# A list scheduler that weighs the remaining chain, and earlier gates for the first weight slabs

## The reference, cut to what matters

```python
def reference(x, ...):                                   # x: (4, 4096, 1024) float32, one layer
    h = rmsnorm(x, norm_mix_g)
    q, f, i, g, c_gate, b_gate, xb, gate_a, gate_b = jnp.split(h @ w_in, offsets, axis=-1)
    y_a = hgrn2_mixer(q, f, i, g, lb, hg_norm_g) @ w_branch_a    # gated linear recurrence, 4 heads,
                                                                 # state 128 x 128 per head
    y_b = (b_gate * causal_conv3(c_gate * xb)) @ w_branch_b
    x = x + (sigmoid(gate_a) * y_a + sigmoid(gate_b) * y_b) @ w_out
    h2 = rmsnorm(x, norm_ffn_g)
    x = x + (silu(h2 @ w_ffn_gate) * (h2 @ w_ffn_up)) @ w_ffn_down       # hidden width 2816
    return rmsnorm(x, norm_final_g)
```

## Time and profile before

| | |
|---|---|
| time, median of 3 runs (lowest to highest) | 1033.21 us (1032.44 to 1033.33) |
| the profiled execution's own time | 1035.37 us |
| its span, slowest core (core 3) | 1033.8 us |
| spans of the eight cores | 1024.6 to 1033.8 us |
| PE busy on core 3 | 1000.4 us, 97% |
| DVE, ACT busy on core 3 | 470.1 us, 406.5 us |
| HBM read, written | 100.16 MB, 16.78 MB |

### The profile page before, as it was taken

The page is one execution under the profiler, slowest core; times in us unless marked ns, Lnnn a source line. Parts: engine busy times, 40 slices in busy tenths (PEclk is TensorE's granted clock), DMA queues, the critical chain, the costliest instruction groups (busy, mean ns, idle before and its releaser), DMA issues.

```text
span 1033.8 us, 15076 instructions; the slowest of 8 cores (1024.6 to 1033.8 us)
## 1 busy us (share of the span) xinstructions
PE 1000.4 (97%) x5446; PEld 489.0 (47%) x5446; DVE 470.1 (45%) x666; ACT 406.5 (39%) x690; POOL 23.2 (2%) x49
## 2 busy tenths in 40 slices
PE   4799999999999999999999999999999999999997
PEld 4465545454555545444444444444444444444444
DVE  5686565476777776446564332121212121232223
ACT  3786553676767675233433231111111111111112
POOL 2000000000000000000000000000000000000000
PEclk9899999999999999999999999999999999999999
DMA  9973324024000261723329444020403116222211
GB/s 193 216 205 122 103 62 82 1 30 95 1 1 2 41 115 49 119 86 123 119 86 180 133 95 82 1 41 1 82 1 59 24 28 194 103 104 102 82 61 62
DMA packets 20232, 84.87 MB, mean 82 GB/s; under 512 B 2368, under 2 KB 2368, under 8 KB 16960
## 3 DMA queue, kind: packets, MB, share of 16 engines
q0 software_dynamic: 5904, 33.03, 18.5%
q1 hardware_dynamic: 14112, 50.62, 14.4%
q10 hardware_dynamic: 144, 0.26, 0.1%
HBM read 100.16 MB, written 16.78 MB: 113 GB/s over the span
## 4 chain that ended last, share of the span: by engine, by line
PE 89%; DMA 5%; issue 2%; DVE 2%; ACT 2%; SPq 0%; POOL 0%; ACTq 0%; DVEq 0%; POOLq 0%
PE pf L736 59%; PE pf L1304 15%; PE pf L745 10%; DMA arena<-x_main 2%; PE pf L763 2%; DMA ring<-x_prev 1%; DMA ring<-wall 1%; ACT arena L714 1%; PE pf L969 1%; PE pf L794 1%; DVE arena L863 1%; DVE arena L718 0%; PE pf L1122 0%; PE pf L829 0%; PE pf L1168 0%
## 5 line engine op out<-in xcount | busy, mean ns | idle before, releaser
L736 PE MATMUL pf<-hT,ring 128*128 128x512 bf16 x2560 | 573.5, 380 | 2.2 <-ACT arena L714 1.8
L736 PEld LDWEIGHTS pf<-hT,ring 128*128 128x128 bf16 x2560 | 249.4, 98 | 298.6 <-issue 4.1
L1304 PE MATMUL pf<-ring,arena 128*128 128x512 bf16 (+1 forms) x726 | 152.2, 373 | 0.0
L714 ACT ACTIVATE arena<-pf 128x512 f32<-128x512 f32 (+3 forms) x164 | 99.3, 641 | 102.7 <-PE pf L736 84.8
L714 ACT ACTIVATE rtmp<-pf 128x512 f32<-128x512 f32 (+1 forms) x89 | 52.8, 593 | 176.5 <-PE pf L736 176.4
L1304 PEld LDWEIGHTS pf<-ring,arena 128*128 128x128 bf16 x726 | 71.0, 98 | 81.2
L718 DVE TENSOR_TENSOR arena<-rtmp,pf 128x512 bf16<-128x512 f32 (+1 forms) x69 | 46.9, 679 | 134.8 <-PE pf L736 130.0
L745 PE MATMUL pf<-ring,arena 128*128 128x512 bf16 x384 | 92.6, 389 | 5.0 <-DMA ring<-wall 4.8
L736 PE MATMUL pf<-arena,ring 128*128 128x512 bf16 x320 | 79.7, 379 | 1.0 <-ACT arena L714 1.0
L714 ACT ACTIVATE rtmp<-hT 128x1024 bf16<-128x1024 f32 (+2 forms) x18 | 17.3, 962 | 123.7 <-DVE hT L718 123.7
L745 PEld LDWEIGHTS pf<-ring,arena 128*128 128x128 bf16 x384 | 37.9, 100 | 50.5 <-issue 10.2
(11 more groups left out here) (99 smaller groups left out, 667.8 us busy)
## 6 DMA issues: line engine op xcount, KB each, us to landing
ring<-wall POOLq DMA_DIRECT2D x25, 1024.0 KB, 10.7
ring<-x_prev SPq DMA_DIRECT2D x16, 512.0 KB, 6.9
ring<-x_main SPq DMA_DIRECT2D x16, 512.0 KB, 4.4
arena<-x_main SPq DMA_DIRECT2D x16, 512.0 KB, 4.6
x1spill<-arena SPq DMA_DIRECT2D x16, 512.0 KB, 2.9
hT<-x1spill SPq DMA_DIRECT2D x16, 512.0 KB, 3.6
out<-hT SPq DMA_DIRECT2D x15, 512.0 KB, 2.7
ring<-wall POOLq DMA_DIRECT2D x6, 512.0 KB, 6.5
```

Of the source, the lines that this page charges most:

```text
L714: P.op("act", lambda E: E.activation(out=rs(out), in_=rs(in_), func=func, **kw), reads=reads, writes=writes, dur=dur, aset=ASET[func] if f ...
L736: last = E.matmul(pb(bk)[:, 0:ncol], lhsT=sl[:, o_:o_ + 128], rhs=rhs[:, c, :], start=(c == 0), stop=(c == kc - 1))
L1304: last = E.matmul(pb(bk)[:, 0:w], lhsT=act_v(c)[:, n * 128:(n + 1) * 128], rhs=rl[c], start=(c == 0), stop=(c == 21))
```

## The change

The scheduler's `prio` was the index in program order. It is now that index less `TAIL_WEIGHT` (1.0) times `tail`, the longest chain of durations, in us, from the operation to the end of the program by dependencies alone, hand-overs and DMA times included. The estimates change: `DMA_RATE` 310 to 295 GB/s, the hand-over to PE 0.15 to 0.8 us (`PE_SLACK`), eight transposes 0.7 to 0.48 us, the 32 narrow matmuls of `halo_gen` 2.0 to 0.9 us. In `pick` an operation that isn't the oldest must leave an aligned pair of banks free, not just any two, and a single bank goes to a half-used pair where times tie; the oldest PE operation is always a candidate. The gates change: all four quarters of f go at once; quarters 0 and 1 of i wait for x tile 1, and 2 and 3 for x tile 2 (before: tiles 1, 2, 3, 3); x tiles 4 to 7 wait for the quarters 0 to 3 of i (before: tile 4 for tile 3, tile 5 for the last quarter of f, tiles 6 to 9 for the quarters of i). No instruction of computation is added or removed.

```diff
@@ -101,8 +101,10 @@
                  "fin", "pos", "extra", "prio")
 
 
-DMA_RATE = 310.0e3
+DMA_RATE = 295.0e3
 DMA_LAT = 2.2
+PE_SLACK = 0.8
+TAIL_WEIGHT = 1.0
 
 
 class Prog:
@@ -178,6 +180,11 @@
         for o in ops:
             for d in o.deps:
                 ops[d].succ.append(o.i)
+        tail = [0.0] * len(ops)
+        for o in reversed(ops):
+            t = max([tail[j] + 0.15 for j in o.succ], default=0.0)
+            tail[o.i] = t + (o.dur if o.chan is None else DMA_LAT + o.nbytes / DMA_RATE)
+            o.prio = o.i - TAIL_WEIGHT * tail[o.i]
         order = {e: [] for e in ENGS}
         t_eng = {e: 0.0 for e in ENGS}
         avail = {e: [] for e in ENGS}
@@ -195,17 +202,19 @@
                 avail[o.eng].append(o.i)
 
         def pick(n, oldest):
-            nfree = sum(1 for h in held if not h)
-            if nfree - n < (0 if oldest else 2):
-                return None
             best = None
             for k in range(0, nbanks - n + 1, n):
                 if any(held[k:k + n]):
                     continue
+                if not oldest:
+                    rest = [h or k <= j < k + n for j, h in enumerate(held)]
+                    if not any(not rest[j] and not rest[j + 1] for j in range(0, nbanks, 2)):
+                        continue
                 t = max(bank_free[k:k + n])
-                if best is None or t < best[0]:
-                    best = (t, k)
-            return best
+                key = (t, n == 1 and not held[k ^ 1])
+                if best is None or key < best[0]:
+                    best = (key, k)
+            return None if best is None else (best[0][0], best[1])
 
         while left:
             while head_pe < len(pend_pe) and pend_pe[head_pe] in done_pe:
@@ -215,6 +224,8 @@
                 if not avail[e]:
                     continue
                 cand = sorted(avail[e], key=lambda i: ops[i].prio)[:window]
+                if e == "pe" and head_pe < len(pend_pe) and pend_pe[head_pe] in avail[e] and pend_pe[head_pe] not in cand:
+                    cand.append(pend_pe[head_pe])
                 rows = []
                 for i in cand:
                     o = ops[i]
@@ -276,7 +287,7 @@
             for j in o.succ:
                 q = ops[j]
                 q.need -= 1
-                q.ready = max(q.ready, o.fin + (0.06 if q.eng == e else 0.15))
+                q.ready = max(q.ready, o.fin + (0.06 if q.eng == e else PE_SLACK if q.eng == "pe" else 0.15))
                 if q.need == 0:
                     avail[q.eng].append(j)
             left -= 1
@@ -668,10 +679,9 @@
         P.op("pool", lambda E: E.memset(idf, 0.0), writes=[b_idf])
         P.op("pool", lambda E: E.affine_select(out=idf, in_=idf, pattern=[[-1, 128]], compare_op=ALU.not_equal, fill=1.0,
                                                base=0, channel_multiplier=1), reads=[b_idf], writes=[b_idf])
-        load_next([None, None, xm[0], xm[1]], 4)
-        load_next([xm[1], xm[2], xm[3], xm[3]], 4)
-        xgate.update({4: xm[3], 5: b_ring[slot_of["f"]][3]})
-        xgate.update({6 + q: b_ring[slot_of["i"]][q] for q in range(4)})
+        load_next([], 4)
+        load_next([xm[1], xm[1], xm[2], xm[2]], 4)
+        xgate.update({4 + q: b_ring[slot_of["i"]][q] for q in range(4)})
         for _ in range(2):
             load_more()
         mskf, b_mskf = Wt[:].rearrange("p h d -> p (h d)")[:, 0:128], b_W
@@ -762,7 +772,7 @@
                 for c in range(8):
                     last = E.transpose(out=tbv.res()[:, c * 128:(c + 1) * 128], in_=xs[:, c * 128:(c + 1) * 128], identity=ident[:])
                 return last
-            P.op("pe", tr, reads=[b_xs, b_ident], writes=[tb.buf], dur=0.7)
+            P.op("pe", tr, reads=[b_xs, b_ident], writes=[tb.buf], dur=0.48)
             tt(dst[:, :, t * 128:(t + 1) * 128], tbv.rearrange("p (c t) -> p c t", t=128),
                cst[:, gcol:gcol + 8].rearrange("p (c o) -> p c o", o=1).to_broadcast([128, 8, 128]), ALU.mult,
                [tb.buf, b_cst], b_dst)
@@ -891,7 +901,7 @@
                     for n in range(8):
                         last = E.transpose(out=tbv.res()[:, n * 128:(n + 1) * 128], in_=kT[kb][:, n * 128:(n + 1) * 128], identity=ident[:])
                     return last
-                P.op("pe", tr, reads=[b_kT[kb], b_ident], writes=[tb.buf], dur=0.7)
+                P.op("pe", tr, reads=[b_kT[kb], b_ident], writes=[tb.buf], dur=0.48)
                 for q in range(2):
                     src = tbv[:, q * 512:(q + 1) * 512].rearrange("p (t d) -> p t d", d=128)
                     dst = ktp[:, :, (2 * pr + q) * 128:(2 * pr + q + 1) * 128]
@@ -930,7 +940,7 @@
                             last = E.matmul(pb(bk)[:, m * 2:m * 2 + 2], lhsT=sl[:, o_:o_ + 128], rhs=hcol[:, c, :],
                                             start=(m == 0 and c == 0), stop=(c == 7), skip_group_check=True)
                     return last
-                P.op("pe", fn, reads=b_sl + [b_hcol], writes=[bk.buf], dur=2.0)
+                P.op("pe", fn, reads=b_sl + [b_hcol], writes=[bk.buf], dur=0.9)
                 yield 1.5
             i = cyc("p1s", P1S)
             cs = single(i)
```

## The result

| | before | after |
|---|---|---|
| median on the same chip | 1032.83 us | 1039.93 us |
| ratio after to before, 95% interval | | 1.0063, 1.0046 to 1.0081 |
| span of the slowest core | 1033.8 us | 1036.5 us (core 7) |
| spans of the eight cores | 1024.6 to 1033.8 us | 1028.7 to 1036.5 us |

The change makes the kernel slower by 0.6%, 6.5 us; the forecast was 6.3 us faster. Some executions of any version show one die's cores at a lower granted clock than the other's; all ratios leave these out, and the numbers of e11 by core are from the other die. The profiled execution of after took 1038.06 us, the lowest of its runs, and that of before 1035.37, above its median, so the traces show only 2.7 of the 6.5 us.

A forecast was written before the change was run, and what follows sets the result against it. PE, busy 97% of the span, bounds, with only the first 140 us to win. Slow cores' clock -5.8, further start gain -1.0, low stretch +1.5, order -1.0: -6.3, from 1033.2 to 1026.9 us; range 1019 to 1036.

The forecast's parts named there:

- The gain of the start: Start: slab i earlier, slow cores keep their clock (-5.8), a further part passes (-1.0), one low stretch stays (+1.5 us).
- Order in the first 140 us: First stage: chain work pulled forward on ACT and DVE wins some PE idle time, -1.0 us (bounds -4.5 and +3).
- From 140 us on: 0: After 140 us: no change, PE covered by ready matmuls; the 2.33 us wait at 578 us is left.
- Rival D: Stage 3 slab loads: two x tiles fall behind slabs, slower, 1037 us; chance 0.19 with other late losses of order.
- The longer hand-over is a plan's margin: All stages: free while PE has other ready work, else up to 0.65 us a hop.
- Plus at most about one later tile: Start: beyond f, i and tiles 0 to 3 (6.3 MB), one later tile slips in before i completes, 1.8 us.
- my 25.5: Start: the time in us by which slab i would be complete.
- The slow cores then come to where core 1 is: -5.8: First 140 us: PE doesn't idle between f and i, the clock need not fall, slow cores gain 5.8 us.
- Rival B: Start: the clock stays low on one core of eight through the v tiles, gain only 1 to 3 us; chance 0.15.
- The term of one low stretch: Start: one low-clock stretch left on the slowest core, priced by eight matmuls at 3.31 us, +1.5 us (bounds 0 and +4.5).
- Two of the signs named for being wrong: Wrong if slow cores still show a clock of 0.992, or PE idles more than 4 us beyond 140 us.
- f's end: Start: f complete by some 10 us, tile 3 in place at 25.5, 32 matmuls remain, ending at 27.3 us.

The follow-up runs named there:

- e11: The kernel after with the hand-over to PE back at 0.15 us, chain weight kept: ratio 1.0103 to the kernel before.
- e2: The kernel after with the gates of before: ratio 1.0061 to the kernel before.
- e9: The kernel after with only the planner's landing time of x tile 13 set 13.3 us later: ratio 0.9984 to the kernel before.
- e7: The kernel before with the second and third slab loads of stage 3 waiting for x tiles 13 and 14: ratio 0.9944, 1029.1 us.
- e13: The kernel before with only the planner's landing time of x tile 13 set 13.3 us later: ratio 0.9948 to the kernel before.
- e10: The kernel before with the hand-over to PE counted as 0.8 us, nothing else: ratio 1.0066 to the kernel before.
- e14: e12 with the gates of before: ratio 1.0000 to the kernel before.
- e12: The kernel after without chain weight, hand-over 0.15 us, second and third slab loads of stage 3 behind x tiles: ratio 0.9964 to the kernel before.
- e4: The kernel after with the second and third slab loads of stage 3 waiting for x tiles 13 and 14: ratio 0.9985 to the kernel before.
- e1: The kernel after with no chain weight (TAIL_WEIGHT 0): ratio 1.0067 to the kernel before.

## Why the prediction was wrong

Between the forecast, 6.3 us faster, and the measured 6.5 us slower lie 12.8 us, and three steps of the sum share them. The gain of the start, -5.8 - 1.0 + 1.5, didn't come: the gates are worth nothing in after (e2). Order in the first 140 us, put at -1.0, came as some +4.2, the constants included. And "From 140 us on: 0" came as +2.3. Each of these is uncertain by about 2 us.

**"From 140 us on: 0".** It was argued from the cover by ready matmuls, and the wait at 578 us was left as it was. On core 7 PE is busy 854.32 us from 140 to 1000, against 857.38, 2.3 of the 3.1 in stage 3. Rival D named the right place, with 0.19, and the wrong mechanism: it had two tiles fall behind the slabs because loads are moved. The load takes as long as it did. The chain weight pulls the transposes of tiles 12 and 13 forward in PE's list, which the plan allows because it has tile 13 land 10.4 us after its issue and not 19.2 to 22.5; the list then has 16 matmuls, 3.5 us, less ahead of them. e9, with the loads untouched, shows it. The price has two terms: 4.83 us of wait and 2.0 of clock on core 7, where before had 2.33 and 1.7. I had left the second pair as it was; by e7 and e13 it was worth 5.4 to 5.8 us to the kernel before.

**"The longer hand-over is a plan's margin ... It costs nothing as long as PE has other ready work."** The condition isn't met from 60 to 140 us. The estimate also isn't a delay of up to 0.65 us a hop, my bound: it changes which operation PE takes, and waits of 1.6 and 3.2 us appear. Alone it costs 6.8 us (e10). My bounds for the whole of order, -4.5 to +3, were too narrow on the side of loss. The durations, `DMA_RATE` and the bank rule, which I put at 0 or inside these bounds, cost 5.8 us between e7 and e14.

**"Plus at most about one later tile".** I counted 6.3 MB ahead of i and one tile more. Core 7 of after, the chain of waits up to the v tiles, and then the issues of SP:

```profile
13.23 17.71 DMA ring<-wall
...
31.08 1.01 PE pf L755 x2
```

```profile
17.26 0.33 SPq L669 DMA_DIRECT2D ring<-x_prev  x1
20.71 0.33 SPq L669 DMA_DIRECT2D ring<-x_prev  x1
21.14 0.56 SPq L669 DMA_DIRECT2D ring<-x_prev  x1
23.19 0.33 SPq L669 DMA_DIRECT2D ring<-x_prev  x1
25.67 0.33 SPq L669 DMA_DIRECT2D ring<-x_prev  x1
31.01 0.33 SPq L669 DMA_DIRECT2D ring<-x_prev  x1
```

The last quarter of i loads for 17.71 us, and five x tiles are issued into that time; the sixth issue comes 0.07 us after the quarter has landed. Four further tiles at 1.8 us each are 7.2 us, more than the 5.6 by which 31.08 misses my 25.5. Each x gate opens as soon as a quarter has landed, so tiles 4 to 6 go between the quarters. The other two are tiles 8 and 9, which the new gates leave free: the trace doesn't name them, but the scheduler's list of after has tiles 8, 9, 4, 5, 6 and 7 in this order. The v tiles start 0.9 us earlier at the median of the cores, instead of 2.9 to 4.15, and on the last of them not at all (31.63 us, before 31.45). I had also left out that `prio` orders SP's own issues, the constants among them.

**"The slow cores then come to where core 1 is: -5.8."** It hung on the slab. PE still stands idle ahead of the v tiles, the clock still falls on five of eight cores (before, on four), and the spans are 7.8 us apart (before 9.2). Rival B's picture of the start, clock and all, is what came, though not its gain of 1 to 3 us. The term of one low stretch, 3.31 us for eight matmuls, has the right size: it is what each wait brings.

**What was right, and what was luck.** No engine that bounds has more work. Two of the signs named for being wrong came: a core with a clock of 0.992, and more than 4 us without work for PE beyond 140 us (5.7). f's end at 26.9 us (27.3) is luck: tile 3 came 2.5 us earlier than I priced it, and three times the matmuls were left, because the last quarter of f landed at 18.8 us and not by some 10. To have the quarters of f issued at once, the first part of the gates' change, didn't move that landing (19.1 before). The gates gain 3.7 us in e12, of which the slab's 0.6 us is the part that I had forecast; in after they gain nothing (e2).

**The account of the 6.5 us,** by differences of ratios, each uncertain by about 2 us: stage 3 costs after 8.1 us and before 5.8, so 2.3 more; the constants 1.7 to 1.9; what is left, some 2.4 us, is order in the first 140 us (core 7: 74.86 us busy from 60 to 140, core 3 of before 76.21) and wasn't separated further. Open: which part of the change makes which loss there, and why weight and hand-over together do better than either alone. The lists differ in too many places for one experiment to name the operation.

The best version is e7, the kernel before with the second and third slab load behind x tiles: 0.9944, 1029.1 us, and e13 with 0.9948 can't be told from it. None of the versions with parts of the change beats it.

## What to carry to other kernels

In a kernel whose engines run fixed lists, a landing time that the planner has wrong costs only what the work in front of it doesn't cover, and a new priority can use up that work: compare the planned landings with the trace first, above all of small loads beside bulk loads, and correct those (for one number 5.4 us in e13, with the old priority, and 8.2 us in e9, with the new one). A pessimistic estimate isn't a safe one, since an in-order engine pays for the other order it causes; and a priority by remaining chain must not push a small load that everything needs behind large ones. When a scheduler's rule is changed, forecast the losses of order stage by stage, with a width of several microseconds, wherever the engine that bounds has no spare work.

## What the runs showed of the hardware

A load of 512 KB on SP's queue, issued within 3 us of three slabs of 2 MB on POOL's, took 19.2 to 22.5 us on the eight cores of after (before: 18.3 to 23.2), against a median of 4.6 for the sixteen loads of this kind; beside one slab (e4, core 7) the same load took 10.5. The Trainium skill, DMA: Bandwidth & Descriptors, section Queues, rings and completion order, says that the DMA engines take turns between queues that have work. As an estimate, by half of the 0.285 MB/us that the start read, 0.52 MB would take 3.7 us. The measured 19 to 23 us decide: the load didn't get half of the bytes. Whether the turns were uneven or the packets were, no run here shows.

A load of 20 KB behind three tiles of 512 KB on the same queue took 11.9 us (11.3 to 12.3 on the eight cores of after); behind one, with the same gates, 3.3 to 4.6 us (e1). Its size was the same: what stood ahead of it made it late.

A wait of PE can cost more than its length. Eight 128x512 matmuls took 3.57 us behind a wait of 3.30 us (e1, core 5) and 3.57 behind 3.20 (e10), at 1.89 otherwise, but after 1.5 us on core 5 of e12 the clock stayed at its full level. In the rows above, waits of 2.3 to 4.8 us cost 0.6 to 2.9 us more behind them, and not on every core: core 1 of before kept its clock after 3.39 us.
